# Dilated attention done in steps behind the projection tiles of the next head group, with two PSUM banks for the projection

## The reference

```
h    = rms_norm(x, g_mix)
proj = h @ w_in        # rq rk rv rg | dq dk dv | gate_ret gate_dil
ret  = retention(rq, rk, rv) * silu(rg)              # 8 heads
dq, dk = rotary(dq), rotary(dk)                      # 12 heads of 128
dil  = dilated_attention(dq, dk, dv)
x    = x + (sigmoid(gate_ret) * (ret @ w_br_ret)
            + sigmoid(gate_dil) * (dil @ w_br_dil)) @ w_out
```

## Time and profile before

| | |
|---|---|
| Median of 3 executions | 4730.65 us (4725.55 to 4736.2) |
| The profiled execution | 4737.4 us, its span 4735.6 us |
| Mean granted PE clock | 0.958 of full speed |
| PE / PEld busy | 4394.2 us (93%) / 3679.7 us (78%) |
| DVE / ACT / POOL busy | 2613.2 us (55%) / 1731.0 us (37%) / 3294.6 us (70%) |

### The profile page before, as it was taken

How to read it: one execution, slowest core, us unless ns; L and a number is a source line. 1 busy time by engine, 2 the same in 40 slices (tenths; PEclk the granted TensorE clock), 3 DMA queues, 4 the chain that set the end, 5 groups by cost and what they waited for, 6 DMA issues and landing times.

```text
span 4735.6 us, 65884 instructions
## 1 busy us (share of the span) xinstructions
PE 4394.2 (93%) x24574; PEld 3679.7 (78%) x24574; DVE 2613.2 (55%) x3813; ACT 1731.0 (37%) x1875; POOL 3294.6 (70%) x1312
## 2 busy tenths in 40 slices
PE   8898988789999989996998998999999899999997
PEld 1676755678888878884887786889888788888876
DVE  3325775355545664314244512398867856875784
ACT  1234422333333343431543432443333333333433
POOL 0347740678888877881876783797887787788776
PEclk9998979889999999997999999999999999999999
DMA  8346750445445544551544452444454454454443
GB/s 312 123 183 243 300 189 9 151 161 183 180 179 184 181 157 160 184 186 45 187 177 142 166 189 98 169 170 161 177 185 171 159 186 172 161 180 177 173 163 125
DMA packets 111109, 804.92 MB, mean 170 GB/s; under 512 B 12903, under 2 KB 13192, under 8 KB 14088
## 3 DMA queue, kind: packets, MB, share of 16 engines
q1 hardware_dynamic: 108720, 787.30, 45.8%
q10 hardware_dynamic: 2200, 14.90, 0.9%
HBM read 800.06 MB, written 2.10 MB: 169 GB/s over the span
## 4 chain that ended last, share of the span: by engine, by line
PE 41%; POOL 29%; issue 21%; DVE 8%; ACT 1%; DMA 1%; POOLq 0%; DVEq 0%; SPq 0%; ACTq 0%
POOL w_lo L427 28%; PE psum L495 18%; PE psum L497 9%; PE psum L610 3%; PE psum L552 2%; DVE out_hl L2679 2%; DVE out_hl L2677 1%; DVE hid L2675 1%; POOL ada_acc L455 1%; PE psum L1104 1%; PE psum L593 1%; PE psum L484 1%; PE psum L595 1%; PE psum L594 1%; PE psum L485 1%
## 5 line engine op out<-in xcount | busy, mean ns | idle before, releaser
L427 POOL TENSOR_TENSOR w_lo<-ring,w_hi 128x1024 fp32r<-128x1024 f32 x1216 | 2944.3, 2425 | 1286.4 <-ACT w_hi L1180 1285.5
L1180 ACT ACTIVATE w_hi<-ring 128x1024 fp32r<-128x1024 f32 x1240 | 1310.2, 1060 | 2146.8 <-PE psum L497 1887.6
L495 PE MATMUL psum<-hc_hl,w_hi 128*128 128x512 f32 x5184 | 1852.6, 401 | 86.4 <-DVE hc_hl L2138 24.5
L497 PE MATMUL psum<-hc_hl,w_lo 128*128 128x256 f32 x5184 | 1453.8, 280 | 0.0
L495 PEld LDWEIGHTS psum<-hc_hl,w_hi 128*128 128x128 f32 x5184 | 982.0, 189 | 325.3 <-issue 55.9
L497 PEld LDWEIGHTS psum<-hc_hl,w_lo 128*128 128x128 f32 x5184 | 985.8, 190 | 2.0 <-issue 1.9
L495 PE MATMUL psum<-out_hl,w_hi 128*128 128x512 f32 x2048 | 725.0, 398 | 30.3 <-DVE x L2689 27.4
L497 PE MATMUL psum<-out_hl,w_lo 128*128 128x256 f32 x2048 | 577.5, 282 | 0.0
L495 PEld LDWEIGHTS psum<-out_hl,w_hi 128*128 128x128 f32 x2048 | 387.6, 189 | 123.1 <-DVE x L2689 28.3
L497 PEld LDWEIGHTS psum<-out_hl,w_lo 128*128 128x128 f32 x2048 | 390.7, 191 | 0.0
L495 PE MATMUL psum<-hid_hl,w_hi 128*128 128x512 f32 x1024 | 367.0, 402 | 19.6 <-DVE hid_hl L2192 12.2
(11 more groups left out here) (440 smaller groups left out, 5559.1 us busy)
## 6 DMA issues: line engine op xcount, KB each, us to landing
ring<-stream SPq DMA_DIRECT2D x652, 1024.0 KB, 4.8
ring<-mixed SPq DMA_DIRECT2D x96, 1024.0 KB, 6.3
x<-x ACTq DMA_DIRECT2D x2, 2048.0 KB, 11.2
ctx_raw<-ctx ACTq DMA_DIRECT2D x1, 2048.0 KB, 9.8
mem_raw<-mem ACTq DMA_DIRECT2D x1, 2048.0 KB, 7.8
out<-x SPq DMA_DIRECT2D x4, 512.0 KB, 2.6
filt_w<-filt_w ACTq DMA_DIRECT2D x1, 1024.0 KB, 11.0
dft<-dft ACTq DMA_DIRECT2D x1, 1024.0 KB, 12.9
```

Source lines behind the costliest of these rows:

```text
L427: pool.tensor_tensor(w_lo[:, slot], ring[:, s, k], w_hi[:, slot].bitcast(F32), ALU.subtract).then_inc(lo_ready, 1)
L495: pe.matmul(psum[:, b, :].rearrange("p (s t) -> p s t", s=2), w_hi[:, slot, c], x_hl, start=start(c), stop=False, skip_group_check=True)
L497: m = pe.matmul(psum[:, b, 0:T], w_lo[:, slot, c], x_hl[:, 0], start=False, stop=stop(c), skip_group_check=True)
L1180: act.activation(w_hi[:, 2 * (s % 2) + h], ring[:, s, k], ACT.Copy).then_inc(hi_ready, 1)
```

## The change

The dilated tiles come in another order: not all q, all k and all v, but four blocks of nine tiles, block h holding q, k and v of head h for the three patterns. `dil_attention(n)` on PE and `dil_attended(n)` on DVE are called after every tile n (counted through `dil` into `gate`), and do a small piece each: the rotations of the block that is being projected, and the two attention steps of the block before. The last head's pieces stand behind the first gate tiles. ACT's exponentials stand behind its weight splits. The main products use PSUM banks 0 and 1 in turn (`n % 2`), so that banks 2 to 7 serve the attention; a tile now waits for the eviction of tile n-2 (`free` = 3) where it waited for that of tile n-4. The loops of both stages are written out, the last two gate tiles use banks 2 and 3, some buffers have other places, and the load of `mem_raw` is issued after gate tile 7. The arithmetic is the same.

```diff
+DIL_BLOCK = 3 * DIL_G
+DIL_SLOTS = [list(range(8, 17)), list(range(17, 24)) + [32, 33]]
+ROTATE_AT = [(5, 6, 7), (2, 4, 6)]
...
-    pd = at("pd", [P, DIL_TILES, T], 120)
-    v_dil = at("v_dil", [P, 2, DIL_H, P], 156)
+    pd = at("pd", [P, 34, T], 120)
+    v_dil = at("v_dil", [P, 2, DIL_G, P], 162)
-    dil_s = at("dil_s", [P, 2, DIL_G * T], 174)
+    dil_s = at("dil_s", [P, 2, DIL_G * T], 144)
...
+        def tile_in(name, n, bank, free):
+
+            pe.wait_ge(bank_free, bank_of[name] + n + free)
+            for h in range(2):
+                half_wide(FIRST[name] + n, n % RING, h, lambda c: h == 0 and c == 0,
+                          lambda c: h == 1 and c == KC // 2 - 1, lambda c: bank, lambda c: h_hl[:, :, h * 8 + c])
...
-        linear("dil", h_hl)
-        pe.wait_ge(bank_free, 4 + bank_of["gate"])
-        rotate_pe(pd[:], PERM_ROT, 8, 12)
-        turn_v_pe(pd[:, 24:36], 12, 4)
-        pe.wait_ge(rot_d, 20)
-        pe.wait_ge(v_nat_, 10)
...
+        def dil_rotate(h, p):
+            pe.wait_ge(bank_free, 4 + bank_of["dil"] + DIL_BLOCK * h + 2 * p + 2)
+            if p == 0 and h:
+                pe.wait_ge(v_nat_, 4 + 2 * h)
+            if p:
+                pe.wait_ge(rot_d, 8 + 3 * h + p)
+            n = DIL_SLOTS[h % 2][2 * p]
+            pe.matmul(psum[:, 2, :], sq(PERM_ROT), pd[:, n:n + 2].rearrange("p k t -> p (k t)"),
+                      start=True, stop=True).then_inc(rot_p, 1)
+        def dil_turn_v(h, tb):
+            pe.wait_ge(bank_free, 4 + bank_of["dil"] + DIL_BLOCK * h + DIL_BLOCK)
+            if tb:
+                pe.wait_ge(v_nat_, 4 + 2 * h + 1)
+            else:
+                pe.wait_ge(rot_d, 8 + 3 * h + 3)
             for g in range(DIL_G):
-                o = flat[:, 512 * b + T * g:512 * b + T * g + keys]
-                m = pe.matmul(o, pd[:, 4 * g + h, tb * P:tb * P + P], pd[:, 12 + 4 * g + h, 0:keys], start=True, stop=True)
+                m = pe.transpose(psum[:, 2, g * P:g * P + P], pd[:, DIL_SLOTS[h % 2][6 + g], tb * P:tb * P + P], sq(IDENT))
+            m.then_inc(v_tp, 1)
+        def dil_scores(h, tb):
+            m_, keys = 2 * h + tb, P * (tb + 1)
+            pe.wait_ge(rot_d, 8 + 3 * h + 3)
+            if m_:
+                pe.wait_ge(d_mx, m_)
+            for g in range(DIL_G):
+                q_, k_ = (pd[:, DIL_SLOTS[h % 2][i]] for i in (g, DIL_G + g))
+                m = pe.matmul(flat[:, 512 * 3 + T * g:512 * 3 + T * g + keys], q_[:, tb * P:tb * P + P], k_[:, 0:keys],
+                              start=True, stop=True)
             m.then_inc(d_sc, 1)
-        dil_scores(0)
-        for m_ in range(2 * DIL_HG):
-            h, tb = m_ // 2, m_ % 2
-            if m_ + 1 < 2 * DIL_HG:
-                dil_scores(m_ + 1)
+        def dil_turn(h, tb):
+            m_ = 2 * h + tb
             pe.wait_ge(d_p, m_ + 1)
+            if m_:
+                pe.wait_ge(d_pt, m_)
             for g in range(DIL_G):
                 for s in range(tb + 1):
                     n = g * (tb + 1) + s
-                    m = pe.transpose(flat[:, n * P:n * P + P], dil_s[:, m_ % 2, T * g + P * s:T * g + P * s + P],
-                                     sq(IDENT))
+                    m = pe.transpose(flat[:, 512 * 5 + n * P:512 * 5 + n * P + P],
+                                     dil_s[:, m_ % 2, T * g + P * s:T * g + P * s + P], sq(IDENT))
             m.then_inc(d_tp, 1)
+        def dil_out(h, tb):
+            m_ = 2 * h + tb
             pe.wait_ge(d_pt, m_ + 1)
-            if tb == 0 and h >= 2:
-                pe.wait_ge(d_lo, h - 1)
+            pe.wait_ge(v_nat_, 4 + m_ + 1)
+            if tb == 0 and h:
+                pe.wait_ge(d_lo, h)
             last = DIL_G * (tb + 1) - 1
             for n in range(last + 1):
                 g, s = n // (tb + 1), n % (tb + 1)
-                m = pe.matmul(psum[:, 2 + h % 2, tb * P:tb * P + P], v_dil[:, s, 4 * g + h], dil_pt[:, n],
-                              start=n == 0, stop=n == last)
+                m = pe.matmul(psum[:, 7, tb * P:tb * P + P], v_dil[:, s, g], dil_pt[:, n], start=n == 0, stop=n == last)
             m.then_inc(d_o, 1)
-        pe.wait_ge(d_lo, DIL_HG)
-        linear("gate", h_hl)
+        def dil_attention(n):
+            b, t = n // DIL_BLOCK, n % DIL_BLOCK
+            if 0 < b <= DIL_HG:
+                if t == 0:
+                    dil_turn_v(b - 1, 0)
+                    dil_scores(b - 1, 0)
+                if t == 1:
+                    dil_turn_v(b - 1, 1)
+                if t == 2:
+                    dil_turn(b - 1, 0)
+                    dil_scores(b - 1, 1)
+                if t == 3:
+                    dil_out(b - 1, 0)
+                if t == 4:
+                    dil_turn(b - 1, 1)
+                if t == 5:
+                    dil_out(b - 1, 1)
+            if b < DIL_HG and t in ROTATE_AT[b > 0]:
+                dil_rotate(b, ROTATE_AT[b > 0].index(t))
+        for n in range(DIL_TILES):
+            tile_in("dil", n, n % 2, 3)
+            dil_attention(n)
+        for n in range(GATE_TILES):
+            if n < GATE_TILES - 2:
+                tile_in("gate", n, n % 2, 3)
+            else:
+                tile_in("gate", n, n - GATE_TILES + RING, 1)
+            dil_attention(DIL_TILES + n)
...
+        def dil_exp(h, tb):
+            m_, keys = 2 * h + tb, P * (tb + 1)
             act.wait_ge(d_mx, m_ + 1)
             s, n = (t_[:, m_ % 2] for t_ in (dil_s, dil_n))
             s = s.rearrange("p (g k) -> p g k", g=DIL_G)[:, :, 0:keys]
             act.activation(s, s, ACT.Exp, bias=n[:, 0:1], accum_out=n[:, 1:2]).then_inc(d_e, 1)
...
-        act.wait_ge(d_lo, DIL_HG)
-        act.dma_start(mem_raw[:], a["mem"]).then_inc(norm_in, 16)
-        g_gate = FIRST["gate"]
...
+        def dil_high(h):
+            act.wait_ge(d_o, 2 * h + 2)
+            act.activation(dil_hi[:, h], psum[:, 7, 0:T], ACT.Copy).then_inc(d_hi, 1)
+        def gate_sigmoid(n):
+            act.wait_ge(pg_scaled, n + 2)
+            act.activation(pg[:, n], pg[:, n], ACT.Sigmoid).then_inc(s_sig, 1)
+        for n in range(DIL_TILES + GATE_TILES):
+            split_at(FIRST["dil"] + n + 2)
+            if n == 5:
+                act.wait_ge(gn_out, 2)
+                act.dma_start(dil_mask[:], a["dil_mask"]).then_inc(s_tab, 16)
+            b, t = n // DIL_BLOCK, n % DIL_BLOCK
+            if 0 < b <= DIL_HG:
+                if t in (0, 2):
+                    dil_exp(b - 1, t // 2)
+                if t == 5:
+                    dil_high(b - 1)
+            if n == DIL_TILES + 7:
+                act.wait_ge(d_lo, DIL_HG)
+                act.dma_start(mem_raw[:], a["mem"]).then_inc(norm_in, 16)
+            if n >= DIL_TILES:
+                gate_sigmoid(n - DIL_TILES)
...
+        def dil_evict(n):
+            b, t = n // DIL_BLOCK, n % DIL_BLOCK
+            dve.wait_ge(half_done, 2 * (FIRST["dil"] + n) + 2)
+            both(pd[:, DIL_SLOTS[b % 2][t]], n % 2).then_inc(bank_free, 1)
+        def dil_rotated(h, p):
+            n = DIL_SLOTS[h % 2][2 * p]
+            dve.wait_ge(rot_p, 8 + 3 * h + p + 1)
+            if h or p:
+                dve.wait_ge(rot_d, 8 + 3 * h + p)
...
+        def dil_v(h, tb):
+            dve.wait_ge(v_tp, 4 + 2 * h + tb + 1)
+            if tb == 0 and h:
+                dve.wait_ge(d_o, 2 * h)
+            dve.tensor_scalar(v_dil[:, tb].rearrange("p g c -> p (g c)"), psum[:, 2, 0:DIL_G * P],
+                              r_col[:, MIX, tb:tb + 1], None, ALU.mult).then_inc(v_nat_, 1)
+        def dil_scaled(h, tb):
+            m_, keys = 2 * h + tb, P * (tb + 1)
+            if m_ == 0:
+                dve.wait_ge(s_tab, 32)
+            dve.wait_ge(d_sc, m_ + 1)
+            if m_ >= 2:
+                dve.wait_ge(d_tp, m_ - 1)
+            ps = flat[:, 512 * 3:512 * 3 + DIL_G * T].rearrange("p (g k) -> p g k", g=DIL_G)[:, :, 0:keys]
+            st.did(dve.scalar_tensor_tensor(s, ps, P ** -0.5, dil_mask[:, tb, :, 0:keys], ALU.mult, ALU.add))
+            st.settle()
+            dve.tensor_reduce(dil_n[:, m_ % 2, 0:1], s, AX.XY, ALU.max, negate=True).then_inc(d_mx, 1)
+        def dil_prob(h, tb):
+            m_ = 2 * h + tb
+            dve.wait_ge(d_e, m_ + 1)
+            st.did(dve.reciprocal(dil_n[:, m_ % 2, 2:3], dil_n[:, m_ % 2, 1:2]))
+            st.settle()
+            dve.tensor_scalar(s, s, dil_n[:, m_ % 2, 2:3], None, ALU.mult).then_inc(d_p, 1)
+        def dil_turned(h, tb):
+            m_, n = 2 * h + tb, DIL_G * (tb + 1)
+            dve.wait_ge(d_tp, m_ + 1)
+            if m_:
+                dve.wait_ge(d_o, m_)
+            dve.tensor_copy(dil_pt[:, 0:n].rearrange("p n t -> p (n t)"),
+                            flat[:, 512 * 5:512 * 5 + n * P]).then_inc(d_pt, 1)
+        def dil_low(h):
+            dve.wait_ge(d_hi, h + 1)
+            dve.tensor_tensor(dil_lo[:, h], psum[:, 7, 0:T], dil_hi[:, h].bitcast(F32), ALU.subtract).then_inc(d_lo, 1)
+        def dil_attended(n):
```

(32 more changed lines are left out.)

124 lines of the change are left out of this document (17 added, 107 removed).

## The result

The changed kernel takes 4667.52 us (median of 4 executions, 4655.94 to 4672.0), the kernel before 4728.93 us beside it (4 executions, 4725.55 to 4736.2). The ratio is 0.9858, with a 95% interval of 0.9841 to 0.9875: 1.4% faster. The forecast was 4667 us.

A forecast was written before the change was run, and what follows sets the result against it. PE was taken to set the pace in dil and gate, with a chain filling no engine in the attention hole between. -103.7 + 32.1 + 7.1 + 1.0 = -63.5 us from the median 4730.65 gives 4667 us, range 4656 to 4687.

The forecast's parts named there:

- The hole: Attention alone between dil and gate, a chain with no engine full; removing it with its restart saves 103.7 us.
- The pieces: Attention work between PE's tiles, paid in full: 300 units of 128 columns at 0.107 us, 32.1 us.
- Two banks: Late evictions at the start of dil, with two banks instead of four: 1.0 us, 2.1 at most.
- The slower tile: Tiles of dil and gate from the first transposes on: 59 tiles slower by 0.12 us each, 7.1 us.
- Rival 1: Same mechanism, but dil and gate tiles keep 5.55 us: saving 70.6 us, 4660 us; chance 0.18.
- DVE hidden: Heaviest behind t = 2: DVE's 6.5 us fit beside PE's tiles, with a cover of about 5 us; nothing paid.
- ACT hidden: Splits behind exponentials, at worst 2 to 3 us late behind gate tile 2, have 5 us of slack; nothing paid.
- The sum: All terms over dil and gate together: -63.5 us, giving 4667 us from the median; chance 0.60.
- Rival 2: DVE late behind POOL, two banks too few: PE loses about 20 us, saving 43, 4687 us; chance 0.14.
- Rival 3: Pieces wait for each other between tiles as in the hole: 63.5 us given back, 4731 us; chance 0.03.
- Rival 4: ACT's late splits starve POOL and PE behind every exponential: at 9 us each, slower, 4739 us; chance 0.05.

The follow-up runs named there:

- experiment 2: Changed kernel with every PE instruction of the attention pieces issued twice: 4702.43 us, ratio 0.9928.
- experiment 3: Kernel before, attention still in the hole, with only two PSUM banks and written-out dil and gate loops: 4734.75 us, ratio 0.9997.
- experiment 4: Changed kernel with three unused DVE sums of 4096 elements behind t = 2 of each attention block: 4731.36 us, ratio 0.9991.
- number 7: Changed kernel with 1, 3, 5 and 7 unused DVE sums of 1024 elements behind t = 2 of the four blocks: 4687.79 us, ratio 0.9899.
- experiment 5: Changed kernel with output pieces directly behind the turned probabilities, without the tile of lag: 4689.84 us, ratio 0.9904.
- experiment 8: Changed kernel with 4, 8, 12 and 16 unused ACT copies behind the exponential at t = 2 of the four blocks: 4673.35 us, ratio 0.9869.
- number 1: Changed kernel plus one unused 512-column PE product behind gate tile 6: 4660.19 us, ratio 0.9838.
- number 10: Changed kernel plus one unused 512-column PE product behind gate tile 16: 4661.53 us, ratio 0.9843.
- number 11: Changed kernel plus one unused 512-column PE product behind gate tile 6, run again with 5 executions: 4666.11 us, ratio 0.9841.
- number 9: Changed kernel plus one unused 128-column PE product behind gate tile 6: 4670.09 us, ratio 0.9857.

## Why the prediction was right

**The hole, -103.7 us.** As predicted: the distance is 5.55 us in place of 109.22, and the clock is 1.00 throughout.

**The pieces, +32.1 us.** The nine distances of a full block (seven with pieces, two without) sum to 58.4 us, against 9 x 5.55 = 49.95: 8.4 us for 75 units, 0.112 us a unit. In this stands the slower rhythm of some of these tiles (next but one). With all slower tiles taken off, the stretch leaves 103.7 - 67.6 - 3.9 = 32.2 us for the 300 units, 0.107 us each, and experiment 2 puts 0.108 us on each of 300 more. The step that priced a unit by `ret`'s tiles was right; what the prediction doubted, that 128-column records would cost clearly more than a mean over longer ones, did not happen. The busy time in the hole, 63.2 us, would have been twice too much.

**Two banks, +1.0 us.** Measured 0: experiment 3, and in the changed kernel the first distances of `dil` are those of before.

**The slower tile, +7.1 us: the term that was mis-sized.** It measured some 3.9 us. I charged 0.12 us for 59 tiles; 37 tiles were slower, by 0.106 us each. They are found by the starts of PE's main products: from the second of a tile's 16 pairs to the last, a pair takes 346.4 to 347.1 ns in a fast tile and 352.1 to 354.3 ns in a slow one. The 26 gate tiles behind the last outputs were slow, and 11 tiles with pieces ahead of them: two behind rotations of the first block, and two or three in each later block. The others, above all the three tiles behind the last rotation of each block, were fast.

The prediction's reason, that "small pieces between tiles seem to leave PE in this slower rhythm", is right in that the rhythm is fast or slow anew behind each piece; but a piece can leave either. The kind of the piece does not decide it. This is a rotation of 512 columns in `ret` of the kernel before, and the second and the last pair behind it, 353.6 ns a pair:

```profile
1803.62 1.02 PE L903 MATMUL psum<-pr,const 128*128 128x512 f32 x2
1804.83 0.39 PE L495 MATMUL psum<-hc_hl,w_hi 128*128 128x512 f32 x1
...
1809.78 0.40 PE L495 MATMUL psum<-hc_hl,w_hi 128*128 128x512 f32 x1
```

And these are outputs of 128 columns in the changed kernel, and the same pairs behind them, 346.4 ns a pair:

```profile
2001.18 0.83 PE L1001 MATMUL psum<-dil_pt,v_dil 128*128 128x128 f32 x6
2002.20 0.40 PE L498 MATMUL psum<-hc_hl,w_hi 128*128 128x512 f32 x1
...
2007.05 0.40 PE L498 MATMUL psum<-hc_hl,w_hi 128*128 128x512 f32 x1
```

Rival 1 (the tile keeps 5.55) held for nearly half of the 68 tiles, and failed in the rest, above all in `gate`.

**DVE hidden.** Right: PE waited 0.5 us for evictions. The operations with two SBUF inputs grew as in `ret`. The changed kernel's range for the rotation's second operation (ns min/median/max; the third took 0.69 us at the median and 2.80 at most):

```profile
L2406 DVE TENSOR_TENSOR rot_d<-pd,trig x12: 680/1957/2567, 1956.4 to 2139.8; 128x512 f32<-128x512 f32 x12
```

The Trainium skill (page SBUF — State Buffer, section "Who interferes with whom") says that a DVE instruction with two SBUF inputs contends with a GpSimd instruction that reads SBUF. The row agrees, 0.68 us growing to 1.96 at the median, and in this kernel it put no price on PE. What the prediction had wrong is what comes first when DVE is late. It named an eviction with too few banks, from about 13 us of work; experiments 4 and 7 show the turn at t = 4 waiting for the probability, with a cover of 4.8 us in the first three blocks, close to the 5 us I had, and 0.5 us in the last; and 2.0 us of added work were enough to use up the 4.8, since operations that had no POOL operation ahead of them in the changed kernel now had one and quadrupled. The margin in work can be smaller than the margin in time. Nor is a late microsecond only "one of PE's": in experiment 4 the 59.4 us of waiting cost 68.8, since the granted clock was 0.50 behind it.

**ACT hidden.** Right: no wait of PE at an exponential. The estimate of 5 us of slack stands between what was measured: about 7 us in `dil`, and 3.8 us at gate tile 2 on top of the two table loads and the sigmoid.

**The sum.** -103.7 + 32.2 + 3.9 + 0 = -67.6 us in the stretch, where I had -63.5. That the forecast of 4667 us met the measured 4667.5 within 1 us is luck: the terms were 4.1 us too cautious, the profiled spans differ by 69.2 us and the medians by 61.4. I can only tie the rest to the stages around, which are unchanged and whose time moves by more than that from profile to profile.

**Rivals 2 to 4.** Rival 2's mechanism (DVE late) did not occur, and would not have been one of banks. Rival 3 was excluded by the lag: without it (experiment 5) each of eight outputs waits 1.8 us, and with the low clock behind the waits 21.4 us come back at an equal tail, where the rival had assumed 2.0 us for each of 31 pieces. Rival 4 needed 9 us at each exponential; experiment 8 shows that ACT would have to be 7 us later in `dil`, and 3.8 us at gate tile 2, before it costs the first.

## What to carry to other kernels

When a chain of small steps over several engines stands alone in a hole, put each step between the tiles of an engine-bound loop with one whole tile between a step and the one that takes it up. What is then paid is the steps' own time on the bound engine, priced by a stage of the same trace that is built so already; the waits and the low clock of the hole vanish. Check the distances before the banks: here one missing tile of lag cost a third of the gain, and two banks in place of four cost nothing. And count what follows a wait too: where PE stood still for 6 or 15 us, it came back at half of its clock.

## What the runs showed of the hardware

The same tile of 16 pairs of matmuls takes 5.55 or 5.65 us at a granted clock of 1.00. Once `dil` ran steadily in the changed kernel, the rhythm changed only where a piece stood between two tiles; behind the last piece it held for 26 tiles. What sets it is open. A single product of 512 columns ended the slow rhythm at once in numbers 1, 10 and 11, and a product of 128 columns did not in number 9. But in `ret` of the kernel before all seven tiles that stand behind a 512-column rotation between 1800 and 1890 us are slow, and in the changed kernel two of the three in the first block; its repetition has one of them fast and the other slow. Outputs of 128 columns left the tiles behind them fast at many places of the changed kernel, and behind the last of them in number 2. In numbers 4, 7 and 8 PE paused in the last block, ran its last outputs of 128 columns after that, and the tail was 5.55 us; it was so too in number 5, and behind the hole of the kernel before. What sets the rhythms in the stages outside the stretch, and what part they have in the 19 us by which those stages differ between profiles, was not looked into.

After a pause PE's granted clock was lower: 0.50 from 2029 to 2034 us in number 4, after 15 us without work, and from 2198 to 2202 us in number 8, after 6.3 us. After the waits of 1.3 us in number 7 it stayed at 1.00.

A sum over a strided view of 4096 elements a partition took 7.3 us on DVE, and one over 1024 elements 2.0 us, where a maximum over 768 adjoining elements takes 0.95 us.
